# Shift columns summed on VectorE, and four unscaled slabs behind each feed-forward norm, in a float32 transformer kernel

## What is computed

```python
h = h + concat(y_attn, y_ret) @ w_out
m = rms_norm(h, ffn_norm_w)
h = h + (silu(m @ w_gate) * (m @ w_up)) @ w_down
# second block: nine modulation vectors come from silu(c) @ w_ada + b_ada
u = rms_norm(h, ffn1_norm_g) * (1 + scale0) + shift0
h = h + 0.5 * gate0 * swiglu(u)
u = rms_norm(h, mix_norm_g) * (1 + scale1) + shift1
h = h + gate1 * mixers(u @ w_mix + b_mix)
u = rms_norm(h, ffn2_norm_g) * (1 + scale2) + shift2
h = h + 0.5 * gate2 * swiglu(u)
```

## Time and profile before

| | before |
|---|---|
| median of 3 runs | 1978.67 us (1978.63 to 1978.91) |
| span of the profiled execution, first to last instruction | 1976.6 us |
| what lies around the span (median less span) | 2.1 us |
| granted TensorE clock, mean | 1.000 of full speed |
| busy: PE, DVE, ACT, POOL | 1965.8, 856.3, 771.2, 610.4 us |
| HBM read | 207.96 MB |

### The profile page before, as it was taken

How to read it: one execution, slowest core, us unless ns; L and a number is a source line. 1 busy time by engine, 2 the same in 40 slices (tenths; PEclk the granted TensorE clock), 3 DMA queues, 4 the chain that set the end, 5 groups by cost and what they waited for, 6 DMA issues and landing times. The chain is left out here.

```text
span 1976.6 us, 27474 instructions
## 1 busy us (share of the span) xinstructions
PE 1965.8 (99%) x9500; PEld 1580.9 (80%) x9500; DVE 856.3 (43%) x1337; ACT 771.2 (39%) x1199; POOL 610.4 (31%) x241
## 2 busy tenths in 40 slices
PE   9999999999999999999999999999999999999999
PEld 6777878888888888888878877777788888888887
DVE  6888673332224443342284445555221363222200
ACT  7544442222223322232266566666422343322211
POOL 0000124444432344444313330000344423444443
PEclk9999999999999999999999999999999999999999
DMA  4111245543332555552212222112233323333322
GB/s 167 54 54 54 80 145 201 191 149 99 102 102 78 191 193 191 194 183 95 90 59 81 75 75 62 56 53 64 65 98 95 103 76 102 100 95 95 109 90 99
DMA packets 56644, 210.76 MB, mean 107 GB/s; under 512 B 6288, under 2 KB 7056, under 8 KB 56592
## 3 DMA queue, kind: packets, MB, share of 16 engines
q1 hardware_dynamic: 56592, 210.08, 33.1%
HBM read 207.96 MB, written 2.10 MB: 106 GB/s over the span
## 5 line engine op out<-in xcount | busy, mean ns | idle before, releaser
L382 POOL TENSOR_TENSOR wlo<-raw,whi 128x1024 fp32r<-128x1024 f32 (+1 forms) x234 | 603.0, 2577 | 1277.3 <-ACT whi L912 1277.3
L430 PE MATMUL bank<-xh,whi 128*128 128x512 f32 x1688 | 668.2, 396 | 3.8 <-DVE wlo L1452 1.3
L430 PE MATMUL bank<-xh,wlo 128*128 128x512 f32 x1688 | 657.9, 390 | 0.0
L430 PE MATMUL bank<-xl,whi 128*128 128x512 f32 x1688 | 657.4, 389 | 0.0
L912 ACT ACTIVATE whi<-raw 128x1024 fp32r<-128x1024 f32 (+1 forms) x298 | 330.6, 1109 | 618.2 <-PE bank L430 605.8
L430 PEld LDWEIGHTS bank<-xh,whi 128*128 128x128 f32 x1688 | 316.9, 188 | 84.7 <-issue 12.7
L430 PEld LDWEIGHTS bank<-xh,wlo 128*128 128x128 f32 x1688 | 316.8, 188 | 67.1
L430 PEld LDWEIGHTS bank<-xl,whi 128*128 128x128 f32 x1688 | 317.1, 188 | 64.2 <-issue 1.0
L430 PE MATMUL bank<-acth,whi 128*128 128x512 f32 x528 | 205.6, 389 | 0.2
L430 PE MATMUL bank<-actl,whi 128*128 128x512 f32 x528 | 205.4, 389 | 0.0
L430 PE MATMUL bank<-acth,wlo 128*128 128x512 f32 x528 | 205.4, 389 | 0.0
(11 more groups left out here) (322 smaller groups left out, 1914.5 us busy)
## 6 DMA issues: line engine op xcount, KB each, us to landing
raw<-w_dram SPq DMA_DIRECT2D x250, 512.0 KB, 3.6
adaw<-ada_dram SPq DMA_DIRECT2D x72, 512.0 KB, 4.3
raw<-wd_dram SPq DMA_DIRECT2D x48, 704.0 KB, 4.0
h<-x_dram SPq DMA_DIRECT2D x4, 512.0 KB, 7.0
out_dram<-h SPq DMA_DIRECT2D x8, 256.0 KB, 3.8
rel<-rel_dram SPq DMA_DIRECT2D x1, 513.0 KB, 6.5
crow<-c_dram SPq DMA_DIRECT2D x1, 512.0 KB, 3.6
gates_raw<-gates_dram SPq DMA_DIRECT2D x1, 384.0 KB, 4.5
```

What stands on the lines that cost most here:

```text
L382: nc.gpsimd.tensor_tensor(wlo[:, s, 0:width], raw[:, s, 0:width], whi[:, s, 0:width].bitcast(F32), ALU.subtract).then_inc(sem("w_lo"), 1)
L430: mm = nc.tensor.matmul(proj[b][:], w[:, s, W], v[:, k, :], start=first and j == 0 and a == 0, stop=last and j == len(chunks) - 1 and a == ...
```

## The change

Four things change. **Shift columns:** the 96 two-column matmuls go. SP loads the slabs that need a column a second time, as float32, into `adaw` and `crow`, which are free by then (four slabs beside the first down projection, six beside the second). DVE multiplies each by the shift vector and sums over the chunks (`shift_sum`, eleven times, the gates included), in front of and between the tiles of the down projections, and PE adds over the partitions with one float32 matmul of two columns of ones for each (`shift_columns`: four after `down0`, seven after `down1`). **Four unscaled slabs** behind norms 1, 2 and 4; for r = 3 slabs 0 and 1 and then the gates. **Eight temporary tiles**, so that DVE scales all chunks before it makes a low part. In the feed-forward norms DVE makes `wlo` of slabs 2 to 5, and POOL begins at slab 6. **The start:** 14 of the 30 matmuls stay, and 30 in fp32r on another tile of ones follow, of 512, 256, 128 and 480 columns.

```diff
-        tmp = (sqn[:, 0, :], sqn[:, 1, :], ssum[:])
+        tmps = sb("tmps", [P, KC, S], F32, nrm)
...
+        UNSCALED = (2, 3, 4, 7)
+        shift_sums = gsil[:].rearrange("p j (a m) -> p (j a) m", m=P)
         def chunk_free(r, c):
-            return ("gates", 1) if r == 3 else ("mm_done", SLAB[FIRST[r]] + 2)
+            return ("gates", 1) if r == 3 else ("mm_done", SLAB[FIRST[r]] + 4)
@@ block.sync: down0, then down1 @@
+            sp.wait_ge(sem("ada_acc"), primed(4 * ADA0))
+            for b in range(2):
+                load_again(SLAB["ff1"] + b, b)
+            for k in range(4):
+                load_down(0, k // 2, k % 2)
+            sp.wait_ge(sem("shift_sum"), 2)
+            for b in range(2):
+                load_again(SLAB["ff1"] + 2 + b, b)
...
+            for k in range(2):
+                load_down(1, 1, k)
+            sp.wait_ge(sem("ada_acc"), primed(NMOD * KC))
+            for n, b in ((SLAB["mlstm"], 0), (SLAB["mlstm"] + 1, 1), (SLAB["ff2"], 2)):
+                load_again(n, b)
+            for k in range(2):
+                load_down(1, 2, k)
+            sp.wait_ge(sem("shift_sum"), 8)
+            for b in range(3):
+                load_again(SLAB["ff2"] + 1 + b, b)
@@ block.tensor @@
-                    if r > 1:
-                        for a, w in enumerate((hi, lo)):
-                            nc.tensor.matmul(bank[5][0:rows, at:at + 2], w(k), shs[:, r - 2, k, :], ...)
...
+            def shift_columns(done, rows):
+                pe.wait_ge(sem("shift_sum"), done)
+                for j, n in enumerate(rows):
+                    mm = nc.tensor.matmul(bank[5][0:n, 2 * j:2 * j + 2], shift_sums[:, j, 0:n], ones[:, 0:2], ...)
+                mm.then_inc(sem("shift_cols"), 1)
...
-            for _ in range(30):
+            for _ in range(14):
                 nc.tensor.matmul(bank[7][:, 0:P], ones[:], ones[:], start=True, stop=True)
+            pe.wait_ge(sem("ones"), 2)
+            for count, at, n in ((8, 0, S), (8, 0, 2 * P), (8, 0, P), (6, 16, 480)):
+                for _ in range(count):
+                    nc.tensor.matmul(bank[7][:, 0:n], yl[:, KC - 1, 0:P], yl[:, KC - 1, at:at + n], start=True, stop=True)
...
             ff_tiles(0)
             down(0)
+            shift_columns(4, (P,) * 4)
             ff_tiles(1)
             down(1)
+            shift_columns(11, (P, P, 96) + (P,) * 4)
@@ block.scalar: norm, ff_first @@
-                    if c in splits:
-                        split(0, 2, SLAB[FIRST[r]] + 2, splits[c], WC)
+                    for k in splits.get(c, ()):
+                        split(0, 2, SLAB[FIRST[r]] + 2, k, WC)
...
-                split(0, 4, n + 2, 2, WC)
+                split(0, 4, n + 2, 3, WC)
+                for p in range(2):
+                    act.wait_ge(sem("evac0"), primed(TILE[f"ff{run}"] // 2 + 1 + p))
+                    ...
+                    nc.scalar.activation(gsil[:, p, :], gsil[:, p, :], ACT.Silu, ...).then_inc(sem("ff_sil"), 1)
                 if run == 0:
                     act.wait_ge(sem("c_in"), 16)
                     nc.scalar.activation(crow[:], crow[:], ACT.Silu).then_inc(sem("c_silu"), 1)
+                for p in range(2):
+                    act.wait_ge(sem("ff_first"), run * 2 + p + 1)
+                    nc.scalar.activation(chunk(acth, p), aprod[:, p, :], ACT.Copy).then_inc(sem("act_hi"), 1)
...
-            FF_SPLITS = {0: 0, 5: 1}
+            FF_SPLITS = {0: (0, 1), 1: (2,)}
@@ block.vector: norm, ff_first, shift_sum @@
-                for c in range(3):
+                for c in range(KC):
                     scaled(c)
+                    if c == 0 and r != 3:
+                        weight_low(0, 2, first, 0)
+                    if c == 5 and r != 3:
+                        weight_low(0, 2, first, 1)
                 for c in range(KC):
                     low(c)
-                    if c == 0 and r != 3:
-                        weight_low(0, 2, first, 0)
-                    if c + 3 < KC:
-                        scaled(c + 3)
-                weight_low(0, 2, first, 0 if r == 3 else 1)
+                    if c == 1:
+                        weight_low(0, 2, first, 0 if r == 3 else 2)
...
+            def ff_first(run, p):
+                n = SLAB[f"ff{run}"] + 2 * p
                 matmuls(n + 1)
+                V.tensor_tensor(gsil[:, p, :], bank[UNSCALED[2 * p]][:], rstd[:], ALU.mult).then_inc(sem("evac0"), 1)
                 matmuls(n + 2)
+                V.tensor_tensor(aprod[:, p, :], bank[UNSCALED[2 * p + 1]][:], rstd[:], ALU.mult).then_inc(sem("evac1"), 1)
+                if p == 0:
+                    weight_low(0, 2, n, 5)
+                dve.wait_ge(sem("ff_sil"), run * 2 + p + 1)
+                V.scalar_tensor_tensor(aprod[:, p, :], aprod[:, p, :], fb[:, 2 * p + 1:2 * p + 2] if run > 0 else 0.0, gsil[:, p, :], ...)
...
+                V.tensor_tensor(dst.rearrange("p (k m) -> p k m", k=KC), src.rearrange("p (k m) -> p k m", k=KC), sh, ALU.mult)
+                V.tensor_reduce(shift_sums[:, slot, 0:width], dst.rearrange("p (k m) -> p m k", k=KC), AX.X, ALU.add)
...
+            add_tiles("down0", 2, 2, lambda m: 1.0, first=1, after=second_pair)
+            dve.wait_ge(sem("shift_cols"), 1)
+            V.tensor_copy(fb[:, 0:4], bank[5][:, 0:8:2]).then_inc(sem("z_bias"), 1)
...
             norm(3, lambda c: scl[:, KC + c:KC + c + 1], shift=3, beside=gates_scaled)
+            matmuls(SLAB["mlstm"] + 2)
+            V.tensor_tensor(qz[:, 0, CONV - 1:], bank[UNSCALED[0]][:], rstd[:], ALU.mult).then_inc(sem("evac0"), 1)
+            V.tensor_scalar(qz[:, 0, CONV - 1:], qz[:, 0, CONV - 1:], fb[:, 4:5], None, ALU.add).then_inc(sem("m_first"), 1)
+            V.tensor_tensor(qz[:, 1, CONV - 1:], bank[UNSCALED[1]][:], rstd[:], ALU.mult).then_inc(sem("m_first"), 1)
```

More of the change, by code:

```diff
@@ L446, in norm_sum_last, with unscaled @@
                                  skip_group_check=True).then_inc(sem("norm_sum"), 1)
-            def unscaled(r, hi, lo, dst, at, j, done, rows=P):
+            def unscaled(r, hi, lo, dst, first, last, done):
                 for k in range(KC):
-                    if j == 0:
+                    if first:
                         pe.wait_ge(sem("z_lo"), primed(KC * r + k + 1))
@@ L742, in mlstm_head @@
                 for s in range(2, 5):
-                    wide("mlstm", hd, 6, s, early=first and s == 2)
+                    wide("mlstm", hd, 6, s, early=first and s < 4, ready=("x_lo", KC * 2) if first and s == 2 else None)
                 for j in range(2):
@@ L1794, in add_tile, with add_tiles @@
                         z_low(r, m, scale_of(r))
-            def add_tiles(name, per, r, gate, first=0):
+            def add_tiles(name, per, r, gate, first=0, low=False, after=lambda: None):
                 if r is not None:
@@ L1800, in add_tiles @@
                     for s in range(2):
[L1801 removed]
+                        add_tile(name, per, r, gate, i, s, low=low)
+                after()
                 with dve.Fori(0, KC // 2 - 1 - first) as i:
@@ L1852, in ff_beside_ada @@
             def ff_beside_ada(run, i, r0, i0):
+                if not i0:
+                    for p in range(2):
+                        ff_first(run, p)
+                    if run == 0:
+                        dve.wait_ge(sem("c_silu"), 1)
                 for jj in range(2):
-                    if i0 or jj:
+                    if i0:
                         ff_product(run, i, i0, jj)
-                    else:
-                        ff_first(run)
-                        if run == 0:
-                            dve.wait_ge(sem("c_silu"), 1)
                     ada_part(i, r0, 2 * jj)
@@ L1917, in _, with last_three @@
             modulations(1, 3, 2, 6)
-            add_tiles("down1", 2, 3, gate(0))
+            shift_sum(1, 2, None, 0, width=96)
+            for b in range(2):
+                shift_sum(1, b, b, 3)
+            shift_sum(2, 3, 2, 1)
+            def last_three():
+                for b in range(3):
+                    shift_sum(2, 4 + b, b, 4 if b < 2 else 2)
+            add_tiles("down1", 2, 3, gate(0), first=1, after=last_three)
+            dve.wait_ge(sem("shift_cols"), 2)
+            V.tensor_tensor(fb[:, 4:6], bank[5][:, 0:4:2], col[:, COL["b_mlstm"]:COL["b_mlstm"] + 2], ALU.add).then_inc(sem("z_bias"), 1)
+            V.tensor_copy(fb[:, 0:4], bank[5][:, 6:14:2]).then_inc(sem("z_bias"), 1)
+            V.tensor_tensor(fb[0:96, 6:7], bank[5][0:96, 4:5], c1("b_gates", rows=slice(0, 96)), ALU.add).then_inc(sem("g_bias"), 1)
             dve.wait_ge(sem("gates_in"), 16)
```

162 lines of the change are left out of this document (71 added, 91 removed).

## The result

The changed kernel takes 1990.63 us (median of 4 runs, 1990.2 to 1991.81), the kernel before 1978.79 us (4 runs, 1978.63 to 1979.08) on the same chip: ratio 1.0061, 95% interval 1.0049 to 1.0073. It is slower by 12 us. The forecast of 1978.1 us was wrong, and its range of 1971.0 to 1983.5 does not hold the result. The profiled execution spans 1988.9 us against 1976.6, 12.3 more.

The account below looks back on a forecast made before the run. PE, busy 99% of the span, was taken as the bound, with savings only from removed matmuls and waits; +0.5 - 1.0 + 1.7 - 2.0 + 0.2 = -0.6 us took 1978.67 to 1978.1 us, range 1971.0 to 1983.5.

Parts of the forecast that it names:

- Start: Opening matmuls before the first slab: about 17 at half pace, costing +0.2 us, bounds 0 to +2.
- Shift columns: Float32 two-column matmuls on PE: 8 passes after down0 cost 1.0 us, 14 after down1 cost 1.7 us.
- Shift sums hidden: DVE's eleven shift sums, up to 5 us each, fit around the down projections' tiles and cost nothing.
- Rival C: DVE's shift sums are not covered and a down tile comes late by some us: 1981 us; chance 0.04.
- Norm 1: First feed-forward norm: PE waits 2.7 us for slab 6's wlo against waits of 2.2 before, +0.5 us.
- Norm 2: Second feed-forward norm: a 2.65 us wait at slab 6 plus 1.0 for columns, against 4.65 before: -1.0 us.
- rival B: In ff0 and ff1 DVE's modulation steps, beside POOL's subtraction, make slab 7 late: 5.2 us, 1983.3 us; chance 0.11.
- Norm 3: mLSTM norm: DVE's chain to slab 3's wlo starts slab 3 at 29.9 us against 28.2: +1.7, bounds +0.5 and +3.
- Norm 4: Last feed-forward norm: same chain as the second, columns already made, 2.65 against 4.65: -2.0 us.

Follow-up runs that it names:

- e2: Changed kernel with an unused tile of 192 bytes behind fb, putting later tiles at the addresses of the kernel before: 1984.05 us.
- e3: Changed kernel with the start of the kernel before (30 fp32 products, those on yl dropped): 1990.14 us.
- e12: Changed kernel with only norm 3 reordered: DVE makes slab 3's wlo right behind the last xl, ACT splits slab 4 earlier: 1991.65 us.
- e14: e13 without e12's reordering of norm 3: 1974.86 us, ratio 0.9982 to the kernel before.
- e13: e6 with two more moves in the feed-forward norms: ACT's silu of slab 4 and DVE's product of slab 7 come earlier: 1974.11 us, ratio 0.9979.
- e9: Kernel before with an unused tile of 64 bytes ahead of every other tile: 1978.56 us, ratio 0.9999.
- e10: Kernel before with 64 unused bytes ahead of raw and 192 behind fb, moving raw and the weights against all moving tiles: 2022.12 us, ratio 1.0218.
- e15: Kernel before with 64 unused bytes ahead of wlo and 192 behind fb, moving wlo alone against the rest: 2006.84 us, ratio 1.0142.
- e4: Changed kernel; in feed-forward norms ACT splits slab 6 behind the first silu, DVE makes slab 5's wlo ahead of the first pair's products: 1997.03 us.
- e5: e4 with loads of slabs 6 and 7 before three ada loads, and DVE's products of slabs 5 and 7 ahead of ada steps: 1984.72 us.
- e6: e5 with e2's filler, e3's start and e12's order in norm 3: 1977.69 us, ratio 0.9996 to the kernel before.
- e1: Kernel before with an unused tile of 64 bytes behind fb: 1984.99 us, ratio 1.0032.
- e7: Kernel before with 128 unused bytes behind fb: 1992.35 us, ratio 1.0068.
- e11: Kernel before with 192 unused bytes behind fb: 1994.33 us, ratio 1.0079.

## Why the prediction was wrong, by its own steps

The forecast was -0.6 us. With the place of the tiles put back (e2) the change costs +5.3; the place adds 6.6. Two things failed, then. Of the +5.3, e2 less before gives by the table +2.0 us in norm 1 (forecast +0.5), +1.6 in `down0` and norm 2 (-1.0), +3.8 in `down1` and norm 3 (+1.7), and -1.9 in norm 4 (-2.0).

- **A term that the sum did not have.** Removing `shs` and widening `fb` was read for its operations alone. That it moves every later tile by 192 bytes, and that PE's spacing depends on it, stood in no row of before, where all moving tiles lie alike. 6.6 of the 12 us; added to the forecast it gives 1984.7, out of the range. What is left without it is out as well, if barely: e2 takes 1984.05 us, and the range ended at 1983.5.
- **Start, +0.2, bounds 0 to +2.** The first slab starts 1.48 later, inside the bounds. The sum took 17 passes at half pace, and in this trace 27 of the 28 ran so; in e2's, with 13 of them, the same code has its first slab at 10.73, 0.12 later than before. The median shows 0.5 at most (e3).
- **Shift columns, 1.0 and 1.7 us.** A little less, inside the bounds: to the next stage's first matmul it is 626.43 - 625.62 = 0.8 us, and 995.93 - 994.51 = 1.4. The Trainium skill ("TensorE: Matmul & The Clock Gate", section "LDWEIGHTS (loading the stationary operand)") gave an estimate of 2.3 us for the 22 passes, and the trace has 2.2, nearer than my 2.7.
- **Shift sums hidden.** Right (e2). Rival C is out.
- **Norm 1, +0.5.** The wait was right: 37.00 against 36.56, +0.44, released by POOL's `wlo`. The sum had no term for the clock behind such a wait: here eight starts follow 0.43 us apart, 1.6 us. The stage lost 2.2.
- **Norm 2, -1.0.** To slab 6 it gained 39.03 - 38.47 = 0.56, with the columns in, and not 1.0: POOL's subtraction for slab 6, next to a step with ada rows that DVE had begun at 660.62, took 2.90 us (661.13 to 664.03) where the sum had 2.4. Then rival B's mechanism took back 1.6: slab 7 waited 1.42 us for the product of slab 5. The rows of the changed kernel, DVE and POOL:

```profile
667.05 3.44 DVE L1888 SCALAR_TENSOR_TENSOR adaw<-adaw,crow 128x1024 f32<-128x1024 f32 x1 [0.66 <-DMA adaw<-ada_dram]
670.42 0.08 DVE L1888 DVE_READ_ACCUMULATOR adaw<-adaw,crow 128x1 f32 x1
670.42 0.68 DVE L1844 TENSOR_TENSOR aprod<-bank,gsil 128x512 f32<-128x512 f32 x1
```

```profile
661.13 2.90 POOL L412 TENSOR_TENSOR wlo<-raw,whi 128x1024 fp32r<-128x1024 f32 x1 [31.75 <-ACT whi L944]
667.01 2.40 POOL L412 TENSOR_TENSOR wlo<-raw,whi 128x1024 fp32r<-128x1024 f32 x1 [2.98 <-ACT whi L944]
```

  The step began 0.04 us behind POOL's subtraction and took 3.44 us, 2.2 more than alone. The Trainium skill ("SBUF — State Buffer", section "SBUF: two separate sides") has VectorE and GpSimd lock their port pair for a whole instruction; this row agrees, with 669.41 as the moment of release. Behind it the matmul of slab 7 is 1.6 us late. The chance of 0.11 was too low, as the margin of under 1 us in that step should have told.
- **Norm 3, +1.7.** Slab 3's start was right (29.63 against 28.20, +1.43, wait 4.31). But I took that start as the end of the chain. The half pace behind it (seven starts 0.43 us apart, and slow ones at both ends) delayed the first head: PE's first `msM` matmul stands 46.1 us behind the norm's start (1040.65 - 994.51), before 43.2 (1029.98 - 986.79). So +2.9 rather than +1.7, within the bound of +3. Taking the wait away gives little back (e12, e14), since the gates' rows on DVE and ACT end almost as late.
- **Norm 4, -2.0.** Right: 37.06 against 39.03, -1.97; no half pace behind its 1.68 us.
- **Small waits for POOL's `wlo` at the start of `down1`**, 0.2 and 0.4 us, had no term.

So the starts of slab 6 and of the mLSTM's slab 3 were forecast to within 0.7 us, and the time was wrong through what the sum left out: the place of operands, the clock behind a wait, and, at slab 7, a rival that was priced right for one slab (1.6 us) and thought unlikely. Of the 5.2 us that it was given for both norms, 1.6 came in norm 2; in norm 1 the half pace ahead of slab 7 covered it, and in e3, where that was missing, slab 7 waited 0.79 us.

## What to carry to other kernels

When a tile is added, removed or resized, print where every later tile begins and keep the distance between weights and moving operands, modulo 256 bytes, as it was; a filler of 192 bytes was worth 6.6 us here, and the whole change, in its best order (e13), 4.3. When PE is freed of work in front of a fixed chain, follow the chain to the next two or three slabs as well, and move behind it everything on those queues that PE does not need (here loads and products of ada rows). Price a wait on PE with the slow matmuls that may follow it, and ask whether the work behind it has another late input before spending effort on it.

## What the runs showed of the hardware

- The distance between two matmul starts depends on how the moving tile lies against the weights' tile, counted modulo 256 bytes: 226.9 ns at 0, 229.1 at 64, 232.5 at 128, 233.5 at 32 and 192, and still 226.9 with every tile 64 bytes further (e9). With all weights 64 bytes off, the whole kernel is 2.2% slower (e10). With `wlo` alone off, the matmul that uses it costs 9 ns more and each of the other two 2 (e15). Other distances, and the reason, stay open.
- Behind a PE wait of 4.3 to 4.6 us the granted clock fell to 0.50 in every trace that had one (after, e2, e3, e4, e5, e14), and starts 0.43 us apart lasted 2.6 to 5.5 us. Behind one of 2.2 or 2.3 us it fell in some (norm 1 of after and e2, norm 2 of e12) and not in others (norm 2 of after and e2, norm 1 of e3 and e12); behind a single one of 1.8 us and less it never fell. The head of norm 3, with waits of 1.4 and 2.3 us one after the other, ran at 0.58 in e12 and at 1.00 in e6 and e13. Each trace is one execution, and it is partly a matter of the execution: those of e14 with a mean clock of 0.998 took 1975.7 to 1976.7 us, those with 0.999 1973.8 to 1975.5, while every execution of before and of its fillers (e1, e7 to e11, e15) shows 1.000. The shares of kernel and chance stay open.
- At the start, the same 28 fp32 products took from 4.8 to 6.1 us in different kernels, by how long the half pace lasted.
- A float32 matmul with two columns takes 0.10 us a pass in a row of them (1.4 us for 14).
